# A third result tile, two semaphores for the adding stores and a new order of loads in the Strassen loop of a float32 encoder kernel

## The chip, the cores and the metric

The kernel runs on one core of one Trainium2 chip, as a single launch. The metric is the device time of one execution in microseconds. Five engines work side by side: TensorE (PE, its weight loads are listed as PEld), VectorE (DVE), ScalarE (ACT), GpSimd (POOL) and SyncE (SP). SP does nothing but ask for transfers and wait; POOL asks for some transfers too. Everything is float32. PE takes its operands as pairs of a high and a low part, and three matmuls (high by high, high by low, low by high) make one product.

## The reference

Two layers over a residual stream of 2048 tokens by 1024 channels. What matters here is the second, odd layer, cut to this:

```python
h = rms_norm(x, g_pre[l]) * (1.0 + scale) + shift
p = h @ w_in_o                      # 1024 -> 3 * 2048: u, v and the gate z
uv, z = gelu(p[..., :4096]), p[..., 4096:]
u, v = uv[..., :2048], layer_norm(uv[..., 2048:], g_ln, b_ln)
mixed = einsum('gij,bnjgc->bnigc', w_s, chunks_of_128(v)) + b_s
y = (u * mixed * silu(z)) @ w_out_o # 2048 -> 1024
x = x + gate * rms_norm(y, g_post[l])
```

## The kernel before

The first layer (projections, gated linear attention, latent attention, output projection) fills the first half of the run and is not touched. Then come two parts of the second layer.

**The v part** (`v_sp`, `v_act`, `v_dve`, `v_pe`) computes v in four column blocks of 512 (n = 0 to 3) by sixteen tiles of 128 tokens (p = 0 to 15). For each tile PE makes 24 matmuls, ACT takes the result out of PSUM with a GELU into one of four slots of the ring `vev` (L2439), DVE takes statistics from it, and SP stores it to memory (L2404). ACT may write a slot only when the store of four tiles earlier has landed. In the last block (n = 3) SP also asks for the first four pieces of weights of the next part (`pair_load`, issued at L2825, waiting at its head for `s_tqs`). That semaphore tells that POOL has finished `part_sums` and `out_sums`: sums of input and weight blocks for the Strassen scheme, done on POOL in the meantime. From p = 9 on SP asks for the first input sums (`part_load`, L2780).

**The Strassen part** (`uz_sp`, `uz_pool`, `uz_act`, `uz_dve`, `uz_pe`) does the other two projections and the output projection with seven block products in place of eight. It has four stages h = 0 to 3: h = 0 and 1 compute u and z, with 16 units each, h = 2 and 3 compute y in two halves of the sum, with 8 units each. A unit j = (h, i, u) is seven products k = 0 to 6 of 12 matmuls, 128x512 each (L3219 to L3221). While PE is in unit j, ACT and POOL make the high and low parts of the weights of the unit after it, product by product (`pair_hi` L2852, `pair_lo` L2856), after POOL has built three sums of the four weight pieces (`pair_sums`, L2830 to L2833) and later a fourth (`pair_last`, L2838). SP loads the pieces in the order 0, 1, 2, 3; piece 2 may be asked for when POOL has made the low part of product 4 of the weights before, and piece 3 when it has made that of product 6.

At the change of stage the input sums in `hTh` and `hTl` are replaced: 28 parts, four for each product. SP loads them through a ring of six tiles (`part_load`), ACT makes the high part (`part_hi`, L2790), DVE the low part (`part_lo`, L2795), which also frees the ring's tile. The last unit of a stage ("ending") and the first of the next ("opening") do this work; parts 12 to 15 are needed by product 3, parts 16 to 19 by product 4.

Stage h = 3 has eight units, called u0 to u7 below. Each gives two result tiles of 128 tokens by 1024 channels, s = 1 and s = 0. DVE takes products out of PSUM into the tile (L3139 and L3157 for s = 1, L3165 and L3183 for s = 0), adds the first half of the sum that SP has loaded (`add_p`, L3087; loads L2898), ACT squares them (`squares`, L3021), POOL makes the reciprocal root (`rstd`, L2969 to L2973), DVE scales the tile (`scale`, L3093), and POOL starts a transfer that adds the tile to `out` in memory (`add_out`, L2982). `free_y` makes DVE wait until the tile's last content has gone. There are two tiles, one for each s. The scratch output of `squares` is the tile `yp` into which SP loads, so that load waits for `squares`. `cnt_y(j, n)` below is n times the number of units of the stage before j.

The order on each engine is that of the code: queues are in order, and a wait holds all that stands behind it.

Of the kernel before, what the change touches and what calls it, by code (L numbers as in the profile page):

```python
# [62 lines left out]
def emit(nc, a, out):  # L63
# [16 lines left out]
    with ExitStack() as ctx:  # L80
# [2319 lines left out]
        def v_sp(sp):  # L2400
            def store(n, p):
                t = v_tile(n, p)
                sp.wait_ge(s_vev, n * NT + p + 3)
                sp.dma_start(sg_v[t * P:(t + 1) * P, ds(n * 512, 512)], vev[:, p % 4, :]).then_inc(s_vst[p % 4], 16)  # L2404
            norm_load(sp, 1, (6,))
            for t in range(4):
                store(0, t)
            norm_load(sp, 1, (7,))
            for t in range(4, 8):
                store(0, t)  # L2410
            sp.wait_ge(s_tp, 64)
            v_load(sp, 1)
            for t in range(8, NT):
                store(0, t)
            with sp.Fori(1, NV - 1) as n:
                v_load(sp, n + 1)
                for t in range(NT):
                    store(n, t)
                    rows = ds(n * (S // 2) + (t * (P // 2) - S // 2), P // 2)
                    sp.dma_start(out[rows, :], x1[rows, :]).then_inc(s_xo, 16)  # L2420
            for p in range(NT):
                store(NV - 1, p)
                if p == 0:
# [149 lines left out]
        zu3 = at("zu3", H0 + 74 * K, [P, 512])  # L2573
        y_tile = [at("y_tile%d" % t, H0 + (18 + 8 * t) * K, [P, 2, 16 * K])[:, :, 0:512] for t in range(2)]
        uT, zT = ([y[:, b, :] for b in range(2)] for y in y_tile)
        E_add = 256 + 48 * 4

        s_tq, E_tq = s_msx, 5 * NT
        s_zw = sem("s_zw")
        s_tqs, E_tqs = sem("s_tqs"), 0  # L2580
# [67 lines left out]
        def is_last(j):  # L2648
            return is_unit(j, 3, PAIRS[3] - 1, 1)
# [208 lines left out]
        def uz_sp(sp):  # L2858
# [41 lines left out]
            def unit(j):  # L2900
# [53 lines left out]
        def uz_pool(pool):  # L2954
# [20 lines left out]
            def add_out(j, s):  # L2975

                h, i, u = j
                if is_unit(j, 3, 0, 0) and s:
                    pool.wait_ge(s_xo, E_xo + 16 * 2 * NT)
                pool.wait_ge(s_tqs, E_add + cnt_y(j, 32, 16 * (1 - s)))  # L2980
                pool.wait_ge(s_oz, E_oz + cnt_y(j, 4, 4 - 2 * s))
                pool.dma_start(out[ds(i * (4 * P) + (2 * u + s) * P, P), :].rearrange("p (b c) -> p b c", b=2), y_tile[s],  # L2982
                               accum_op=ALU.add).then_inc(s_tqs, 16)

            def unit(j):
                if not is_last(j):
                    pair_sums(pool, j, 1)
                if j[0] == 3 and before(j)[0] == 3:
                    add_out(before(j), 1)
                for k in range(7):  # L2990
                    if not is_last(j):
                        pair_lo(pool, j, 1, k)
                        if k == 1:
                            pair_last(pool, j, 1)
                    if k == 0 and j[0] == 3 and before(j)[0] == 3:
                        rstd(before(j), 0)
                    if k == 3 and j[0] == 3 and before(j)[0] == 3:
                        add_out(before(j), 0)
                    if k == 4 and j[0] == 3:
                        rstd(j, 1)  # L3000
            unit_loop(pool, unit)
            final = (3, PAIRS[3] - 1, 1)
            add_out(final, 1)
            rstd(final, 0)
            add_out(final, 0)

        def uz_act(act):
# [3 lines left out]
            def squares(j, s):  # L3011
                tile = (uT, zT)[s]
                for b in range(2):
                    if s:
                        act.wait_ge(s_pa[1], E_pa + cnt_y(j, 2, 2 - b))
                    elif b:
                        act.wait_ge(s_pa[0], E_pa + cnt_y(j, 1, 1))
                    else:
                        act.wait_ge(s_c11, E_c11 + cnt(j, 1, 1 - NU_))
                        act.wait_ge(s_pa[0], E_pa + cnt_y(j, 1, 1))  # L3020
                    act.activation(yp[:, s, b * 512:(b + 1) * 512], tile[b][:, :], ACT.Square, scale=D ** -0.5,  # L3021
                                   accum_out=ossq2[:, 2 * s + b:2 * s + b + 1]).then_inc(s_osq, 1)
# [55 lines left out]
        def uz_dve(dve):  # L3078
            def add_p(j, s, b):

                y = (uT, zT)[s][b]
                dve.wait_ge(s_py[s], E_py + cnt_y(j, 16, 16))
# [6 lines left out]
            def scale(j, s):  # L3089
                dve.wait_ge(s_or, E_or + cnt_y(j, 6, 6 - 3 * s))  # L3090
                for b in range(2):
                    y = (uT, zT)[s][b]
                    dve.scalar_tensor_tensor(y[:, :], y[:, :], ors[:, s:s + 1], gate[:, 1, b * 512:(b + 1) * 512], ALU.mult, ALU.mult  # L3093
                                             ).then_inc(s_oz, 1)

            def free_y(j, s):
# [3 lines left out]
                elif j[0] == 2 or is_unit(j, 3, 0, 0):  # L3100
                    dve.wait_ge(s_ost[s], E_ost + cnt(j, 32, -32 * NU_))
                else:
                    dve.wait_ge(s_tqs, E_add + cnt_y(j, 32, -16 * s))

            def unit(j):
# [59 lines left out]
                dve.tensor_tensor(uT[1][:, :], PS[:, 6, :], zu2[:, :], ALU.add).then_inc(s_zc12, 1)  # L3165
                parts(ending, 12)
                if h == 3:
                    add_p(j, 0, 1)
                    scale(j, 1)
                if h < 2:  # L3170
# [7 lines left out]
                else:  # L3178
# [3 lines left out]
                    else:  # L3182
                        dve.tensor_tensor(uT[0][:, :], PS[:, 2 + u, :], yp[:, 0, 0:512], ALU.add).then_inc(s_c11, 1)  # L3183
                if is_unit(j, 2, 0, 1):
# [5 lines left out]
        def uz_pe(pe):  # L3190
# [33 lines left out]
            def column_sums():  # L3224
                pe.wait_ge(s_vev, NV * NT + 2)
                pe.wait_ge(s_zw, 16)
                for b in range(2):
# [27 lines left out]
        def _(sp):  # L3255
# [14 lines left out]
            sp.wait_ge(s_xo, E_xo + 16 * 2 * NT)  # L3270
            sp.wait_ge(s_tqs, E_add + 16 * NT)

# [139 lines left out]
```

## Time and profile before

| | us |
|---|---|
| median of 3 runs | 3026.44 (3021.3 to 3030.6) |
| profiled execution, its own time | 3029.56 |
| its span | 3027.7 |
| v part, last block, to the first matmul of the Strassen part | 1862 to 1964 |
| Strassen part | 1964 to 3011 |
| stage h = 3, from its first product | from 2822 |

The span runs from the first to the last instruction; the execution's own time is 1.9 us longer. PE is busy for 95% of the span, DVE 58%, ACT 47%, POOL 46%. In a list of the trace, the bracket behind an instruction tells how long its engine had been idle before it and what ended that.

### The profile page before, as it was taken

The numbers are of one execution on the slowest core, as the hardware profiler recorded it, in microseconds if no ns is written. First come the engines' busy times: TensorE is split into PE (matmuls) and PEld (weight loads), VectorE is DVE, ScalarE is ACT, GpSimd is POOL, SyncE is SP. The second block draws the span as 40 slices with busy tenths as digits, with TensorE's granted clock in tenths as the row PEclk, the third lists the DMA queues.
The fourth block names the chain that finished last, engine by engine and source line by source line (L and its number), as shares of the span: only waits on it lengthen the run. The fifth ranks groups of instructions, "written<-read, shape, count | busy, mean of one in ns | idle before, by whom it ended". The sixth has DMA issues, their size and how long they took to land.

```text
span 3027.7 us, 49891 instructions
## 1 busy us (share of the span) xinstructions
PE 2868.3 (95%) x15972; PEld 2383.0 (79%) x15972; DVE 1742.3 (58%) x2909; ACT 1413.1 (47%) x2582; POOL 1382.8 (46%) x1342
## 2 busy tenths in 40 slices
PE   4999999999999999999999999899998999979887
PEld 4768888788788888887878888688887888868675
DVE  6577777865777777773444221255457545662654
ACT  4652255554555555553244111266567556632432
POOL 0212211366333333332322764186776777667685
PEclk8999999999999999999999999999999999989999
DMA  7243355596211121114543455433225332445665
GB/s 268 67 128 103 106 162 165 178 284 187 72 56 57 58 60 57 58 56 142 176 159 135 163 186 175 144 122 109 99 97 181 106 103 97 150 153 181 205 145 106
DMA packets 309365, 397.64 MB, mean 131 GB/s; under 512 B 22820, under 2 KB 201124, under 8 KB 307143
## 3 DMA queue, kind: packets, MB, share of 16 engines
q1 hardware_dynamic: 300072, 367.50, 37.4%
q0 software_dynamic: 9152, 28.31, 3.7%
q8 instruction: 81, 1.33, 0.2%
q14 instruction: 60, 0.49, 0.1%
HBM read 265.05 MB, written 139.07 MB: 133 GB/s over the span
## 4 chain that ended last, share of the span: by engine, by line
PE 68%; POOL 9%; DMA 7%; DVE 6%; issue 6%; ACT 3%; SPq 1%; POOLq 0%; DVEq 0%; ACTq 0%
PE PS L3219 8%; PE PS L3220 8%; PE PS L3221 8%; PE PS L344 4%; PE PS L346 4%; PE PS L345 4%; POOL tq L2699 4%; PE PS L1795 4%; PE PS L1773 4%; DMA hc<-tq 2%; PE PS L1796 2%; PE PS L1763 2%; PE PS L1764 2%; PE PS L1762 2%; PE PS L1766 2%
## 5 line engine op out<-in xcount | busy, mean ns | idle before, releaser
L3219 PE MATMUL PS<-hTh,wc 128*128 128x512 f32 x1344 | 535.2, 398 | 51.0 <-DVE hTl L2795 17.5
L3220 PE MATMUL PS<-hTl,wc 128*128 128x512 f32 x1344 | 530.2, 395 | 0.0
L3221 PE MATMUL PS<-hTh,wc 128*128 128x512 f32 x1344 | 529.6, 394 | 0.0
L2856 POOL TENSOR_TENSOR wc<-wpr,wc 128x512 fp32r<-128x512 f32 x192 | 271.9, 1416 | 203.4 <-ACT wc L2852 203.3
L3219 PEld LDWEIGHTS PS<-hTh,wc 128*128 128x128 f32 x1344 | 256.5, 191 | 111.2 <-issue 37.0
L3221 PEld LDWEIGHTS PS<-hTh,wc 128*128 128x128 f32 x1344 | 256.6, 191 | 54.6
L3220 PEld LDWEIGHTS PS<-hTl,wc 128*128 128x128 f32 x1344 | 256.8, 191 | 52.6 <-issue 0.2
L344 PE MATMUL PS<-hTh,whi 128*128 128x512 f32 x640 | 257.9, 403 | 1.4 <-DVE hTl L298 1.1
L346 PE MATMUL PS<-hTh,wlo 128*128 128x512 f32 x640 | 250.4, 391 | 0.0
L345 PE MATMUL PS<-hTl,whi 128*128 128x512 f32 x640 | 250.2, 391 | 0.0
L1876 ACT ACTIVATE pb__164<-PS,nm,rq 128x512 f32<-128x512 f32 x256 | 197.4, 779 | 104.1 <-DVE nm L1939 104.1
L2856 POOL TENSOR_TENSOR wc<-wsx,wc 128x512 fp32r<-128x512 f32 x144 | 194.7, 1352 | 102.0 <-ACT wc L2852 102.0
L2041 POOL TENSOR_TENSOR diag<-ident,rinv 128x128 f32<-128x128 f32 x64 | 37.9, 592 | 390.0 <-PE PS L1783 285.2
L2523 PE MATMUL PS<-vsh,hTh 128*128 128x512 f32 x512 | 201.1, 393 | 13.8 <-ACT vev L2439 11.7
L1883 ACT ACTIVATE pt<-PS 128x512 fp32r<-128x512 f32 x256 | 139.5, 598 | 154.2 <-PE PS L1773 154.2
L334 POOL TENSOR_TENSOR whi<-wraw,zero 128x1024 fp32r<-128x1024 f32 x18 | 35.3, 1963 | 361.6 <-PE PS L346 361.6
L2524 PE MATMUL PS<-vsl,hTh 128*128 128x512 f32 x512 | 200.2, 391 | 0.0
L2525 PE MATMUL PS<-vsh,hTl 128*128 128x512 f32 x512 | 200.1, 391 | 0.0
L2479 DVE BATCH_NORM_STATS2 vst<-vev 128x6 f32<-128x512 f32 (+1 forms) x64 | 44.3, 693 | 247.0 <-ACT vev L2439 246.8
L1795 PE MATMUL PS<-pt,mvh 128*128 128x512 f32 x512 | 185.4, 401 | 1.1 <-DVE pt L1952 1.1
L1952 DVE TENSOR_TENSOR pt<-PS,pt 128x512 fp32r<-128x512 f32 x256 | 164.0, 682 | 9.8 <-ACT pt L1883 7.7
L371 ACT ACTIVATE pev<-PS 128x512 f32<-128x512 f32 x80 | 47.7, 596 | 258.0 <-PE PS L346 257.4
(320 smaller groups left out, 6919.9 us busy)
## 6 DMA issues: line engine op xcount, KB each, us to landing
wpr<-wuz SPq DMA_DIRECT2D x128, 256.0 KB, 3.4
projT<-pev SPq DMA_DIRECT2D x80, 256.0 KB, 2.7
xt<-x SPq DMA_DIRECT2D x8, 2048.0 KB, 8.5
mw<-wmod SPq DMA_DIRECT2D x64, 256.0 KB, 2.8
sg_v<-vev SPq DMA_DIRECT2D x64, 256.0 KB, 2.7
vm<-sg_v SPq DMA_DIRECT2D x32, 512.0 KB, 3.8
sgT<-mT SPq DMA_DIRECT2D x32, 512.0 KB, 3.5
wpr<-sgT SPq DMA_DIRECT2D x64, 256.0 KB, 3.2
```

What stands on the lines that cost most here:

```text
L344: pe.matmul(PS[:, bank, :], w[1][:, s, k, :], hTh[:, k, b], start=(k == 0), stop=False)
L345: pe.matmul(PS[:, bank, :], w[1][:, s, k, :], hTl[:, k, b], start=False, stop=False)
L346: mm = pe.matmul(PS[:, bank, :], w[2][:, s, k, :], hTh[:, k, b], start=False, stop=(k == KD - 1))
L1795: pe.matmul(PS[:, 6, :], vh[:, tok], pt[:, k, :, :].rearrange("p a q -> p (a q)"), start=(k == 0), stop=False)
L1876: act.activation(pb_[:, u, blk(b)], PS[:, b, :], ACT.Exp, bias=nm[:, u:u + 1], scale=rq2[:, 0, ds(i * 2 + u, 1)], accum_out=rs4[:, u, b:b ...
L2523: pe.matmul(o, hTh[:, k, tok], vsh[:, k, :], start=(k == 0), stop=False)
L2524: pe.matmul(o, hTh[:, k, tok], vsl[:, k, :], start=False, stop=False)
L2525: mm = pe.matmul(o, hTl[:, k, tok], vsh[:, k, :], start=False, stop=(k == KD - 1))
L2856: pool.tensor_tensor(w_part(k, 1), W_SRC[k], w_part(k, 0).bitcast(F32), ALU.subtract).then_inc(s_wcl, 1)
L3219: pe.matmul(o, wc[:, k, 0, kk, :], hh, start=(kk == 0 and not onto), stop=False, skip_group_check=onto)
L3220: pe.matmul(o, wc[:, k, 0, kk, :], hl, start=False, stop=False, skip_group_check=onto)
L3221: mm = pe.matmul(o, wc[:, k, 1, kk, :], hh, start=False, stop=(kk == 3), skip_group_check=onto)
```

## The change

It has six parts.

1. In the last block of the v part, the request for the first four weight pieces moves from behind the store of tile 0 to behind the store of tile 4.
2. In the opening unit of stages 1 to 3, SP asks for piece 2 before parts 12 to 21, and for piece 3 behind them. Before, it was parts 12 to 17, pieces 2 and 3, parts 18 to 21.
3. The s = 0 tile of every second unit of h = 3 is a new tile, `y_next`. It is contiguous in its partition.
4. The adding stores have two semaphores, `s_tqs` for s = 0 and `s_yb` for s = 1, and no longer wait for one another. `free_y` waits for s = 1 of the unit before, and for s = 0 of two units before.
5. POOL starts the s = 0 add of two units before ahead of the loop over k, the s = 1 add of the unit before at k = 0 behind `pair_lo`, and `rstd` for s = 0 at k = 2.
6. DVE scales the s = 0 tile of the unit before behind the sum of the fifth product (k = 4) in place of that of the third, and scales its s = 1 tile before `add_p` of s = 0.

Also, `s_zw` becomes an old semaphore with a base of 128.

```diff
@@ v_sp
             for p in range(NT):
                 store(NV - 1, p)
-                if p == 0:
+                if p == 4:
                     pair_load(sp, (0, 0, 0), range(4), True)
@@
+        y_next = at("y_next", X0 + 52 * K, [P, 2, 512])[:, :, :]
+        def y_of(j, s):
+            return y_next if j[0] == 3 and s == 0 and j[2] else y_tile[s]
@@ uz_sp, unit
-                parts(opening, 12, 18)
                 if not is_last(j):
-                    pair_load(sp, after(j), (2, 3))
-                parts(opening, 18, 22)
+                    pair_load(sp, after(j), (2,))
+                parts(opening, 12, 22)
+                if not is_last(j):
+                    pair_load(sp, after(j), (3,))
@@ uz_pool, add_out
-                pool.wait_ge(s_tqs, E_add + cnt_y(j, 32, 16 * (1 - s)))
                 pool.wait_ge(s_oz, E_oz + cnt_y(j, 4, 4 - 2 * s))
-                pool.dma_start(out[...], y_tile[s], accum_op=ALU.add).then_inc(s_tqs, 16)
+                pool.dma_start(out[...], y_of(j, s), accum_op=ALU.add).then_inc(s_yb if s else s_tqs, 16)
@@ uz_pool, unit
-                if j[0] == 3 and before(j)[0] == 3:
-                    add_out(before(j), 1)
+                if j[0] == 3 and before(j)[0] == 3 and before(before(j))[0] == 3:
+                    add_out(before(before(j)), 0)
                 for k in range(7):
...
                     if k == 0 and j[0] == 3 and before(j)[0] == 3:
+                        add_out(before(j), 1)
+                    if k == 2 and j[0] == 3 and before(j)[0] == 3:
                         rstd(before(j), 0)
-                    if k == 3 and j[0] == 3 and before(j)[0] == 3:
-                        add_out(before(j), 0)
@@ uz_pool, end
+            add_out(before(final), 0)
             add_out(final, 1)
             rstd(final, 0)
             add_out(final, 0)
@@ uz_dve, free_y
-                else:
-                    dve.wait_ge(s_tqs, E_add + cnt_y(j, 32, -16 * s))
+                elif s:
+                    dve.wait_ge(s_yb, cnt_y(j, 16))
+                elif not is_unit(j, 3, 0, 1):
+                    dve.wait_ge(s_tqs, E_add + cnt_y(j, 16, -16))
@@ uz_dve, unit
-                if h == 3 and before(j)[0] == 3:
-                    scale(before(j), 0)
                 parts(opening, 16)
...
                 if h == 3:
                     add_p(j, 1, 0)
+                if h == 3 and before(j)[0] == 3:
+                    scale(before(j), 0)
...
                 if h == 3:
+                    scale(j, 1)
                     add_p(j, 0, 1)
-                    scale(j, 1)
```

On POOL, in a unit of the loop of h = 3 (u2), this stood in a row before: the three sums of the weight pieces (`wsx`, `wpr`), the add of s = 1 (`y_tile1`), the low part of product 0 (`wc`), the reciprocal root (`small`).

```order
L2830 TENSOR_TENSOR wsx_217<-wpr_216 128x512
L2832 TENSOR_TENSOR wsx_217<-wsx_217,wpr_216 128x512
L2833 TENSOR_TENSOR wpr_216<-wpr_216 128x512
L2982 DMA out<-y_tile1_222 256x1x512
L2856 TENSOR_TENSOR wc_207<-wpr_216,wc_207 128x512
L2969 TENSOR_TENSOR small_55<-small_55 128x1
L2971 TENSOR_TENSOR small_55<-small_55 128x1
L2973 TENSOR_TENSOR small_55<-small_55,negh_57 128x1
```

And this stands there now, at the same place (its lines are 6 to 9 higher):

```order
L2836 TENSOR_TENSOR wsx_217<-wpr_216 128x512
L2838 TENSOR_TENSOR wsx_217<-wsx_217,wpr_216 128x512
L2839 TENSOR_TENSOR wpr_216<-wpr_216 128x512
L2988 DMA out<-y_tile0_221 256x1x512
L2862 TENSOR_TENSOR wc_207<-wpr_216,wc_207 128x512
L2988 DMA out<-y_tile1_222 256x1x512
L2862 TENSOR_TENSOR wc_207<-wsx_217,wc_207 128x512
```

Two adds now stand around the first low part, the s = 1 one second; the root has gone behind the low part of product 2.

On DVE, in u1, the second unit of h = 3, the sums of products 1 to 4 (`zu`, then `y_tile1_222`, which is s = 1) stood like this before, with the scaling of s = 0 (`y_tile0_221`) among them:

```order
L3129 TENSOR_TENSOR zu3_220<-PS,zu2_219 128x512
L3093 SCALAR_TENSOR_TENSOR y_tile0_221<-y_tile0_221,small_55,gate_56 128x512 x2
L3139 TENSOR_TENSOR y_tile1_222<-PS,zu3_220 128x512
L3087 TENSOR_TENSOR y_tile1_222<-y_tile1_222,yp_224 128x512
L3157 TENSOR_TENSOR y_tile1_222<-PS,zu2_219 128x512
```

Now the scaling stands behind all of them:

```order
L3138 TENSOR_TENSOR zu3_220<-PS,zu2_219 128x512
L3146 TENSOR_TENSOR y_tile1_222<-PS,zu3_220 128x512
L3094 TENSOR_TENSOR y_tile1_222<-y_tile1_222,yp_225 128x512
L3164 TENSOR_TENSOR y_tile1_222<-PS,zu2_219 128x512
L3094 TENSOR_TENSOR y_tile1_222<-y_tile1_222,yp_225 128x512
L3100 SCALAR_TENSOR_TENSOR y_tile0_221<-y_tile0_221,small_55,gate_56 128x512 x2
L3174 TENSOR_TENSOR y_next_223<-PS,zu2_219 128x512
```

The sum of product 3, for which PE's product 5 waits, now stands directly behind that of product 2.

On SP, at the opening of stage 2 (`hst` are the ring's tiles, `hw` and `woo` the sources of the parts, `wpr` the weight pieces, two at the first place being pieces 0 and 1), before:

```order
L2825 DMA wpr_216<-sgT 128x4x128 x2
L2780 DMA hst4_205<-hw 128x512
L2780 DMA hst5_206<-hw 128x512
L2780 DMA hst0_201<-hw 128x512
L2780 DMA hst1_202<-hw 128x512
L2780 DMA hst2_203<-hw 128x512
L2780 DMA hst3_204<-hw 128x512
L2825 DMA wpr_216<-sgT 128x4x128 x2
L2780 DMA hst4_205<-hw 128x512
L2780 DMA hst5_206<-hw 128x512
```

Now:

```order
L2831 DMA wpr_216<-sgT 128x4x128 x3
L2786 DMA hst4_205<-hw 128x512
L2786 DMA hst5_206<-hw 128x512
L2786 DMA hst0_201<-hw 128x512
L2786 DMA hst1_202<-hw 128x512
L2786 DMA hst2_203<-hw 128x512
L2786 DMA hst3_204<-hw 128x512
L2786 DMA hst4_205<-hw 128x512
L2786 DMA hst5_206<-hw 128x512
```

Piece 2, with its wait for POOL, stands ahead of parts 12 to 17.

## Rows read from the trace of the kernel before

**Rows 1.** The page, part 5: the costliest group of matmuls.

```profile
L3219 PE MATMUL PS<-hTh,wc 128*128 128x512 f32 x1344 | 535.2, 398 | 51.0 <-DVE hTl L2795 17.5
```

**Rows 2.** Timeline of SP, last v block: start, duration, instruction.

```profile
1868.34 0.35 SPq L2404 DMA_DIRECT2D sg_v<-vev  x1
1905.09 1.78 SPq L2825 DMA_DIRECT2D wpr<-wuz  x4
```

**Rows 3.** Timelines of ACT (tiles 4, 5 and 9) and of PE, same stretch.

```profile
1889.48 0.60 ACT L2439 ACTIVATE vev<-PS 128x512 f32<-128x512 f32 x1 [4.84 <-PE PS L2525]
1911.42 0.60 ACT L2439 ACTIVATE vev<-PS 128x512 f32<-128x512 f32 x1 [21.34 <-DMA sg_v<-vev]
...
1931.17 0.60 ACT L2439 ACTIVATE vev<-PS 128x512 f32<-128x512 f32 x1 [4.84 <-PE PS L2525]
...
1912.07 0.80 PE L2523 MATMUL PS<-vsh,hTh 128*128 128x512 f32 x1 [11.75 <-ACT vev L2439]
```

**Rows 4.** Openings of stages 1 and 2: SP and DVE at stage 2, PE at both.

```profile
2641.87 4.77 SPq L2780 DMA_DIRECT2D hst<-hw  x6
2649.55 6.15 SPq L2825 DMA_DIRECT2D wpr<-sgT  x2
...
2650.95 3.18 DVE L2795 TENSOR_TENSOR hTl<-hst,hTh 128x512 fp32r<-128x512 f32 x4 [4.06 <-ACT hTh L2790]
...
2321.87 0.77 PE L3219 MATMUL PS<-hTh,wc 128*128 128x512 f32 x1 [7.93 <-DVE hTl L2795]
...
2666.84 0.77 PE L3219 MATMUL PS<-hTh,wc 128*128 128x512 f32 x1 [9.61 <-DVE hTl L2795]
```

**Rows 5.** Opening of stage 3: SP and PE.

```profile
2824.87 3.10 SPq L2780 DMA_DIRECT2D hst<-hw  x6
2828.01 7.58 SPq L2825 DMA_DIRECT2D wpr<-sgT  x2
2835.69 0.93 SPq L2780 DMA_DIRECT2D hst<-hw  x2
...
2844.30 0.77 PE L3219 MATMUL PS<-hTh,wc 128*128 128x512 f32 x1 [5.94 <-issue]
```

**Rows 6.** Waits of PE from 2850 us to the end: total, times, longest.

```profile
PE PS L3219 <- DVE y_tile L3139: 13.3, 5, 3.5
```

**Rows 7.** Timelines of DVE, SP and POOL in u2 and u3; DVE in u6.

```profile
2894.31 0.68 DVE L3139 TENSOR_TENSOR y_tile<-PS,zu 128x512 f32<-128x512 f32 x1
...
2913.80 3.44 DVE L3093 SCALAR_TENSOR_TENSOR y_tile<-y_tile,small,gate 128x512 f32<-128x512 f32 x2 [4.12 <-POOL small L2973]
2917.16 0.68 DVE L3139 TENSOR_TENSOR y_tile<-PS,zu 128x512 f32<-128x512 f32 x1
...
2984.88 0.68 DVE L3139 TENSOR_TENSOR y_tile<-PS,zu 128x512 f32<-128x512 f32 x1
...
2899.92 3.82 SPq L2825 DMA_DIRECT2D wpr<-sgT  x2
...
2906.07 1.62 POOL L2830 TENSOR_TENSOR wsx<-wpr 128x512 f32<-128x512 f32 x1 [2.87 <-DMA wpr<-sgT]
...
2910.26 1.11 POOL L2982 DMA_DIRECT2D out<-y_tile  x1
...
2912.18 0.67 POOL L2969 TENSOR_TENSOR small<-small 128x1 f32<-128x1 f32 x1
...
2925.78 1.29 POOL L2856 TENSOR_TENSOR wc<-wpr,wc 128x512 fp32r<-128x512 f32 x1 [1.00 <-ACT wc L2852]
```

**Rows 8.** DMA: 3012 to 3020 us in 40 slices; issues, median us to landing.

```profile
DMA  0000000000000000990589899899999998200000
...
wpr<-sgT SPq DMA_DIRECT2D x64, 256.0 KB, 3.2
...
out<-y_tile POOLq DMA_DIRECT2D x16, 512.0 KB, 5.8
```

**Rows 9.** Timeline of POOL: the last add of the program.

```profile
3019.72 1.11 POOL L2982 DMA_DIRECT2D out<-y_tile  x1 [3.49 <-DMA out<-y_tile]
```

More of the change, by code:

```diff
@@ L2574, in emit @@
         y_tile = [at("y_tile%d" % t, H0 + (18 + 8 * t) * K, [P, 2, 16 * K])[:, :, 0:512] for t in range(2)]
+        y_next = at("y_next", X0 + 52 * K, [P, 2, 512])[:, :, :]
         uT, zT = ([y[:, b, :] for b in range(2)] for y in y_tile)
         E_add = 256 + 48 * 4
+        def y_of(j, s):
+            return y_next if j[0] == 3 and s == 0 and j[2] else y_tile[s]
         s_tq, E_tq = s_msx, 5 * NT
-        s_zw = sem("s_zw")
+        s_zw, E_zw = s_ox[1], 128
+        s_yb = sem("s_yb")
         s_tqs, E_tqs = sem("s_tqs"), 0
@@ L2979, in add_out @@
                     pool.wait_ge(s_xo, E_xo + 16 * 2 * NT)
-                pool.wait_ge(s_tqs, E_add + cnt_y(j, 32, 16 * (1 - s)))
                 pool.wait_ge(s_oz, E_oz + cnt_y(j, 4, 4 - 2 * s))
-                pool.dma_start(out[ds(i * (4 * P) + (2 * u + s) * P, P), :].rearrange("p (b c) -> p b c", b=2), y_tile[s],
-                               accum_op=ALU.add).then_inc(s_tqs, 16)
+                pool.dma_start(out[ds(i * (4 * P) + (2 * u + s) * P, P), :].rearrange("p (b c) -> p b c", b=2), y_of(j, s),
+                               accum_op=ALU.add).then_inc(s_yb if s else s_tqs, 16)
             def unit(j):
@@ L3011, in squares @@
             def squares(j, s):
-                tile = (uT, zT)[s]
+                tile = y_of(j, s)
                 for b in range(2):
@@ L3020, in squares @@
                         act.wait_ge(s_pa[0], E_pa + cnt_y(j, 1, 1))
-                    act.activation(yp[:, s, b * 512:(b + 1) * 512], tile[b][:, :], ACT.Square, scale=D ** -0.5,
+                    act.activation(yp[:, s, b * 512:(b + 1) * 512], tile[:, b, :], ACT.Square, scale=D ** -0.5,
                                    accum_out=ossq2[:, 2 * s + b:2 * s + b + 1]).then_inc(s_osq, 1)
@@ L3079, in add_p @@
             def add_p(j, s, b):
-                y = (uT, zT)[s][b]
+                y = y_of(j, s)[:, b, :]
                 dve.wait_ge(s_py[s], E_py + cnt_y(j, 16, 16))
@@ L3091, in scale @@
                 for b in range(2):
-                    y = (uT, zT)[s][b]
+                    y = y_of(j, s)[:, b, :]
                     dve.scalar_tensor_tensor(y[:, :], y[:, :], ors[:, s:s + 1], gate[:, 1, b * 512:(b + 1) * 512], ALU.mult, ALU.mult
@@ L3164, in unit @@
                     free_y(j, 0)
-                dve.tensor_tensor(uT[1][:, :], PS[:, 6, :], zu2[:, :], ALU.add).then_inc(s_zc12, 1)
+                dve.tensor_tensor(y_of(j, 0)[:, 1, :], PS[:, 6, :], zu2[:, :], ALU.add).then_inc(s_zc12, 1)
                 parts(ending, 12)
                 if h == 3:
+                    scale(j, 1)
                     add_p(j, 0, 1)
-                    scale(j, 1)
                 if h < 2:
@@ L3182, in unit @@
                     else:
-                        dve.tensor_tensor(uT[0][:, :], PS[:, 2 + u, :], yp[:, 0, 0:512], ALU.add).then_inc(s_c11, 1)
+                        dve.tensor_tensor(y_of(j, 0)[:, 0, :], PS[:, 2 + u, :], yp[:, 0, 0:512], ALU.add).then_inc(s_c11, 1)
                 if is_unit(j, 2, 0, 1):
@@ L3225, in column_sums @@
                 pe.wait_ge(s_vev, NV * NT + 2)
-                pe.wait_ge(s_zw, 16)
+                pe.wait_ge(s_zw, E_zw + 16)
                 for b in range(2):
@@ L3270, in _ @@
             sp.wait_ge(s_xo, E_xo + 16 * 2 * NT)
-            sp.wait_ge(s_tqs, E_add + 16 * NT)
+            sp.wait_ge(s_tqs, E_add + 8 * NT)
+            sp.wait_ge(s_yb, 8 * NT)
         @block.gpsimd
```

## The prediction, made before the result was known

> **What bounds the kernel now.** I read the page first. The costliest matmul group is that of the Strassen part, with 51.0 us of idle time before it [rows 1]. PE is busy nearly everywhere, so what can be won lies in its gaps, and I looked for them in the timeline, from the v part on. Three places bear on the change.
>
> The last v block: PE stands still for 11.75 us, released by an eviction of ACT; ACT itself had been idle for 21.34 us and waited for a store [rows 3]. SP shows why. It issues the store of tile 0 at 1868.34 and the weight pieces only at 1905.09: for 36 us it stands at the wait for POOL's sums, with the stores of tiles 1 to 15 behind it [rows 2]. The ring of four is full after tile 4.
>
> The openings: PE is idle for 7.93, 9.61 and 5.94 us before product 4 of stages 1, 2 and 3 [rows 4, 5].
>
> Stage 3: five waits, 13.3 us in all, for L3139, the sum of product 3 [rows 6]. From u2 to u6 L3139 comes every (2984.88 - 2894.31)/4 = 22.64 us [rows 7], of which PE waits 13.3/5 = 2.7. It is a loop. L3139 at 2894.31 leads over add_p, squares and SP to the request for piece 2 at 2899.92; it has landed when POOL's sums start at 2906.07; 4.19 us later the s = 1 add is issued, then a low part, the root (from 2912.18), the scaling on DVE (from 2913.80), and L3139 at 2917.16 [rows 7]. I call the start of the sums S and that of L3139 X: S to X is 11.09, X to S 11.76.
>
> **Part 1, the request behind tile 4.** Stores 1 to 4 leave at once, so tiles 5 to 8 find their slots free. Tile 9 needs the store of tile 5, which SP issues behind the pieces at 1905.09 + 1.78 = 1906.9. The pace is 4.84 + 0.60 = 5.44 us a tile, so tile 9 is evicted at 1889.48 + 5 x 5.44 = 1916.68 instead of 1931.17 [rows 2, 3]. Gain 14.5 us: the wait, and the slower matmuls behind it (the first takes 0.80 us). What follows is paced by these tiles, so all of it moves. The slack is about 6 us (1916.7 less some 4 for store and landing, against 1906.9); if POOL's sums end later than that, the gain shrinks one for one.
>
> **Part 2, the openings.** Piece 2 could not leave earlier than it did: SP reached it after the six parts, 2641.87 + 4.77 = 2646.6, and issued it at 2649.55 [rows 4], so it waited for POOL, not for the parts. Now the parts wait too, and part 12 leaves at 2650.0 in place of 2641.87. Landing takes about 4.5 us, as between the requests from 2835.69 on and part 18 or 19 of stage 3 [rows 5]. DVE makes parts 12 to 15 from 2650.95 to 2654.1 [rows 4]; now some 4.5 us later. Behind them DVE has four products of the gate, and these lose less since POOL is later too: I take +2.1 of the 4.5 for product 4, and by the same steps +1.8 at stage 1 (bounds 0, if DVE catches up, and 4 each). At stage 3 the six parts leave quickly, 2824.87 to 2828.0, and piece 2 at 2828.01: now they leave 2.7 later. But part 18 stood behind piece 3, at 2835.69 [rows 5], and now needs only a free ring tile, about 1.3 us earlier; it leads to product 4 at 2844.30. I take -1.6 (bounds -3 and +2.7). Together +2.3.
>
> **Parts 3 to 6, the loop.** The root and the scaling leave the path from S to X. What is late next is `free_y` for s = 1: the add of the unit before must have landed. It is issued not at 4.19 but behind another add and a low part, at 4.19 + (2912.18 - 2910.26) = 6.11 [rows 7]. An add alone takes 5.8 us from issue to landing, and for some 3.8 of them, 3015.2 to 3019, the 16 DMA engines are 80 to 99% busy [rows 8]. The trace shows no two adds at once. Bounds: beside the first one, X = S + 6.11 + 5.8 = 11.9; fully behind it, with 0.8 for the weight piece that goes beside them (half the bytes, at most half of the 3.8), S + 4.19 + 5.8 + 3.8 + 0.8 = 14.6. Busy engines speak for the second. For every other add of s = 0 the source is contiguous, which may shorten the first. I take 14.0 on average, near the second bound: +2.9 against 11.09.
>
> X to S gets shorter: the request for piece 2 took 6.15 us beside an add (by the order in the code the s = 0 add went out at k = 3, just ahead of the low part that releases the piece). No add is in flight there now. The median over the run is 3.2 [rows 8], and the load for `yp` still goes ahead of it, so I take 4. Then POOL is next: its low part of product 6 ended at 2925.78 + 1.29 = 2927.07, 9.9 after X [rows 7], and PE's longer gap makes that 10.5. So X to S is 10.5, -1.3. A round costs +1.6, and there are five (u2 to u6): +8.0. Bounds: 11.9 + 10.3 = 22.2, -0.4 x 5 = -2, and 14.6 + 11.9 = 26.5, +3.8 x 5 = +19. The scaling on DVE and the early release of the s = 0 tile are worth nothing: they hang off the loop.
>
> The Trainium skill, "DMA: Bandwidth & Descriptors", section "Anatomy of one DMA — SWDGE (gpsimd) path", gives 2.0 us and the bytes over 436 GB/s; for 512 KB that would be 3.2 us, an estimate, and 1.2 of queue for a second one. The trace disagrees: 5.8 and 3.8 [rows 8]. The same page, section "Two DMAs through the same engine are not ordered", says that descriptors start in order but are pipelined; that speaks for the first bound and is the first rival.
>
> **The end.** The last add waited 3.49 us at 3019.72 for the one before to land [rows 9]. Without that wait it follows the scaling, at about 3017.9: -1.8. Its own landing stays.
>
> **Sum**, on the profiled 3029.56: -14.5 + 2.3 + 8.0 - 1.8 = -6.0, 3023.6. The median of the runs, 3026.4, is 3.1 below that execution, so 3020.4.
>
> **Rivals.**
>
> *The adds overlap.* X = S + 11.9, the loop gains 2 in all instead of losing 8.0: -14.5 + 2.3 - 2 - 1.8 = -16, 3010.4. For it: a busy share does not tell whether an engine could have a second packet under way. Against it: the busy engines [rows 8]. It decides if the second add lands before S + 12.5. Chance 0.25.
>
> *The loop takes all back.* The second add waits fully and piece 2 stays at 6.15, since the load for `yp` ahead of it remains: 26.5 a round, +19; -14.5 + 2.3 + 19 - 1.8 = +5; PE's gaps of 6 us bring slower matmuls as at 1912.07 and 2844.30, and with openings at their upper bounds (+7) it is about +12, 3038. It is slower from +3.5 a round on, that is if the second add lands later than S + 15. Chance 0.13.
>
> *The v stall stays.* If the sums end past 1911 because the stores now share the transfers with them; at full length it leaves +9, 3035. Chance 0.04.
>
> *The openings cost nothing*: 3018.1. Chance 0.10.
>
> *The forecast*, chance 0.48, with its own range 3015 to 3028.
>
> **Numbers.** No change within 0.3%, 9.1 us, can be told from noise: faster means below 3017.3, slower above 3035.5. Faster takes nearly all of the first rival and a little of the forecast and the fourth: 0.33. Slower takes half of the second and some of the third: 0.09, and I allow 0.11. Same 0.56. The range, 3010 to 3035, reaches to the first rival's time and to the last two's.
>
> **What would show it.** Step 1: no gap of PE in the last v block, tile 9's eviction 27.2 us behind tile 4's. Step 2: idle time before product 3 at stages 1 and 2, and product 4 later by about 2 us. Step 3: L3139 released by the add of s = 1, issue to landing near 9 us on the second of a pair, rounds of 24 to 24.5 us; 22.3 would be the first rival, 26 the second. Step 4: the last two adds without a wait between them. The forecast is wrong if the rounds are shorter than before, or if PE still waits for a store of v.

## The result, and the profile after

In 20 runs of each, the changed kernel took 3028.57 us (median; 3023.9 to 3035.2) and the kernel before 3023.20 us (3016.8 to 3031.9): a ratio of 1.0018, with a 95% interval of 1.0010 to 1.0027. That is 5.4 us slower. The prediction said 3020.4, 6.0 below before, in a range of 3010 to 3035. The time lies in the range and inside the 0.3% called "no change", but it went the other way. The profiled execution of the changed kernel took 3031.48 us, with a span of 3029.8 (before: 3029.56 and 3027.7). So the two traces lie 1.9 us apart where the medians lie 5.4 apart: that of before is of an execution 6.4 us above its kernel's median, that of the changed kernel 2.9 above.

The page, part 5, the same group of matmuls as in [rows 1]. Its idle time rose from 51.0 to 63.4 us, and what ends most of it is now the sum of product 3, L3146 (L3139 before):

```profile
L3228 PE MATMUL PS<-hTh,wc 128*128 128x512 f32 x1344 | 538.9, 401 | 63.4 <-DVE y_tile L3146 19.9
```

**The last v block.** Timelines of SP and ACT, the answer to [rows 2, 3]:

```profile
1868.33 16.65 SPq L2404 DMA_DIRECT2D sg_v<-vev  x4
1901.12 1.78 SPq L2831 DMA_DIRECT2D wpr<-wuz  x4
...
1889.46 0.60 ACT L2439 ACTIVATE vev<-PS 128x512 f32<-128x512 f32 x1 [4.84 <-PE PS L2525]
1916.66 0.60 ACT L2439 ACTIVATE vev<-PS 128x512 f32<-128x512 f32 x1 [4.84 <-PE PS L2525]
```

The stores leave as their tiles come, the pieces follow behind tile 4, and tile 9 is evicted at 1916.66, 27.20 behind tile 4. The first matmul of the Strassen part starts at 1949.8 in place of 1964.3.

**The openings.** SP and DVE at the opening of stage 2, then the first matmul of product 4 at stages 1, 2 and 3, as in [rows 4, 5]:

```profile
2630.81 9.89 SPq L2831 DMA_DIRECT2D wpr<-sgT  x3
2640.75 2.88 SPq L2786 DMA_DIRECT2D hst<-hw  x6
...
2646.43 2.63 DVE L2801 TENSOR_TENSOR hTl<-hst,hTh 128x512 fp32r<-128x512 f32 x4 [9.88 <-ACT hTh L2796]
...
2310.36 0.77 PE L3228 MATMUL PS<-hTh,wc 128*128 128x512 f32 x1 [6.44 <-DVE hTl L2801]
...
2661.68 0.77 PE L3228 MATMUL PS<-hTh,wc 128*128 128x512 f32 x1 [8.00 <-DVE hTl L2801]
...
2837.69 0.77 PE L3228 MATMUL PS<-hTh,wc 128*128 128x512 f32 x1 [3.29 <-POOL wc L2862]
```

The three weight pieces are one group on SP, the last of them held until about 2640.3, and parts 12 to 17 start behind it. DVE now stands still for 9.88 us where it did for 4.06. Of the 14.5 us won in the v part, 11.5 are left at product 4 of stage 1 and 5.2 at that of stage 2. The shorter idle time in the row mustn't mislead: part of the wait has only moved ahead of product 3, where a gap of 5.04 us is new at stage 2.

**The loop of stage 3.** Waits of PE from 2850 us on, for [rows 6], then DVE and POOL in u3, for [rows 7]:

```profile
PE PS L3228 <- DVE y_tile L3146: 19.9, 6, 4.2
```

```profile
2891.05 0.69 DVE L3146 TENSOR_TENSOR y_tile<-PS,zu 128x512 f32<-128x512 f32 x1 [7.30 <-DMA out<-y_tile]
...
2915.51 0.69 DVE L3146 TENSOR_TENSOR y_tile<-PS,zu 128x512 f32<-128x512 f32 x1 [7.70 <-DMA out<-y_tile]
...
2966.78 0.69 DVE L3146 TENSOR_TENSOR y_tile<-PS,zu 128x512 f32<-128x512 f32 x1 [8.06 <-DMA out<-y_tile]
...
2991.21 0.69 DVE L3146 TENSOR_TENSOR y_tile<-PS,zu 128x512 f32<-128x512 f32 x1 [6.26 <-DMA out<-y_tile]
...
2901.10 1.29 POOL L2836 TENSOR_TENSOR wsx<-wpr 128x512 f32<-128x512 f32 x1
...
2904.96 0.91 POOL L2988 DMA_DIRECT2D out<-y_next  x1
...
2906.84 1.43 POOL L2988 DMA_DIRECT2D out<-y_tile  x1
```

Every L3146 from u1 on is released by the landing of an add; before, none was. Take S and X as in the prediction. In u3 POOL's sums start at 2901.10 (S), the first add goes at 2904.96, the second at 2906.84, and X is 2915.51: S + 14.4, and 8.67 from the second issue. Over u2 to u6 S to X is 14.3 on average, X to the next S 10.6. From u1 (2866.73) to u6 (2991.21) the five rounds take 124.5 us; before they took 113.0 (from 2871.93 to [rows 7]). The page's list of DMA issues, for [rows 8], shows the landing of the adds at 7.1 us in the median, from 5.8:

```profile
out<-y_tile POOLq DMA_DIRECT2D x12, 512.0 KB, 7.1
```

**TensorE's clock.** Stretches of the loop: length, busy times of PE, PEld, DVE, ACT and POOL, granted clock (1.00 is 2.4 GHz, 0.50 is 1.2 GHz), DMA share, GB/s. First before, u1 to u7, then after: u1 to u7, and the part of u3 behind X.

```profile
2872.00:3004.00 132.00, 118.75 (x498) 96.09 (x498) 67.65 (x80) 42.77 (x92) 107.74 (x109) 0.96 0.60 134
```

```profile
2867.00:3010.00 143.00, 124.64 (x499) 100.67 (x500) 60.06 (x78) 41.77 (x91) 100.20 (x107) 0.92 0.53 122
2915.00:2922.00 7.00, 5.74 (x14) 4.49 (x15) 4.13 (x7) 1.48 (x5) 1.65 (x4) 0.52 0.19 51
```

A mean of 0.96 over 132 us is (1 - 0.96) x 2 x 132 = 11 us at the lower level; 0.92 over 143 us is 23. Behind the longer gaps of PE the products run at half speed for up to 7 us, and POOL, which waits for them through ACT, is busy for 1.65 of the 7. The two rounds with such a long stretch (behind X of u3 and of u5) have the longest X to S, 11.21 both; the others have 10.05 to 10.34. Experiments 3 and 6 below have one stretch of 7 us in their loop each, and there X to S is 11.3, in their other rounds 9.3 to 10.2. The length of the gap alone does not tell: u4 has the longest gap, 4.17 us, and a stretch of 3.5 us.

**The end.** The last add, for [rows 9]: it follows its scaling without a wait for another add.

```profile
3022.42 0.90 POOL L2988 DMA_DIRECT2D out<-y_next  x1 [1.75 <-DVE y_next L3100]
```

From L3146 of u6 to this add it takes 31.2 us, 3.6 less than before. The steps of the two traces add up to the place of the last add: -14.5 (v part), +9.3 (openings, to X of u1), +11.5 (five rounds) and -3.6 (behind them) are +2.7, and the last add goes at 3022.42 in place of 3019.72.

### The profile page after: what moved, and what is told of

It reads as the page before. It is cut to its first block, busy times and chain, and to the rows that moved or that the text cites. A ratio compares the mean times of both kernels' runs of the same rounds, so it can differ in the third digit from the quotient of the medians.

```text
span 3029.8 us, 49875 instructions
## 1 busy us (share of the span) xinstructions
PE 2873.3 (95%) x15972; PEld 2386.9 (79%) x15972; DVE 1741.3 (57%) x2909; ACT 1412.5 (47%) x2582; POOL 1377.7 (45%) x1342
## 4 chain that ended last, share of the span: by engine, by line
PE 76%; issue 6%; DVE 5%; POOL 5%; DMA 3%; ACT 3%; SPq 1%; POOLq 0%; DVEq 0%; ACTq 0%
PE PS L3228 8%; PE PS L3229 8%; PE PS L3230 8%; PE PS L344 4%; PE PS L346 4%; PE PS L345 4%; PE PS L1795 4%; PE PS L1773 4%; PE PS L2523 3%; PE PS L2524 3%; PE PS L2525 3%; PE PS L1796 2%; PE PS L1763 2%; PE PS L1764 2%; PE PS L1762 2%
## 5 line engine op out<-in xcount | busy, mean ns | idle before, releaser
L3228 PE MATMUL PS<-hTh,wc 128*128 128x512 f32 x1344 | 538.9, 401 | 63.4 <-DVE y_tile L3146 19.9
L2858 ACT ACTIVATE wc<-wpr 128x512 fp32r<-128x512 f32 x192 | 119.8, 624 | 105.4 <-PE PS L3230 104.2
```

Source lines behind the costliest of these rows:

```text
L3228: pe.matmul(o, wc[:, k, 0, kk, :], hh, start=(kk == 0 and not onto), stop=False, skip_group_check=onto)
```

## The experiments

Ratios are to the kernel before on the same chip, with 95% intervals. A per cent is 30 us; a difference between two kernels of these tables has an interval of about 0.2%, or 6 us. So times rank the larger effects, and the traces give the sizes of the small ones. A trace is one execution, though, and can lie some way from its kernel's median; where that matters it is said.

**1. Part 1 alone.**

```diff
-                if p == 0:
+                if p == 4:
                     pair_load(sp, (0, 0, 0), range(4), True)
```

> The kernel before with part 1 alone (the four weight pieces asked behind the store of tile 4). Both theories: the v part ends 14.5 us earlier and nothing takes it back, so -14.5 against before, ratio 0.9952. Rival: the stages behind it wait for something that did not move (the openings, or the sums that fill the ring), and part of the 14.5 is lost again; then less than -10.

Measured: 0.9957 (0.9940 to 0.9973), -13 us. Nothing takes the 14.5 back, and the five rounds are as before (22.2 to 23.0 us each, PE waits 13.4 us for L3139). So the rest of the change cost some 18 us.

**2. Parts 1 and 2.** The order of requests is that of the diff above, on the kernel before.

> Parts 1 and 2 (tile 4, and the new order of requests at the openings), the loop of stage 3 as before. The forecast's step for the openings, +2.3, gives -12.2 against before. The reading of the two traces (product 4 lost 3.0 at stage 1, 6.35 at stage 2, and some 2 at stage 3, with 2.9 gained between) gives some +9 for the openings and so -5.5. Ratio 0.9960 by the one, 0.9982 by the other.

Measured: 0.9976 (0.9962 to 0.9990), so the openings cost 0.19%, 5.7 us: above the forecast's 2.3, below the 9 read from one pair of traces, and with an interval of 6 it excludes neither. The trace has the same picture as after (product 4 of stage 2, 350.4 us behind that of stage 1):

```profile
2632.76 9.62 SPq L2825 DMA_DIRECT2D wpr<-sgT  x3
...
2647.66 2.75 DVE L2795 TENSOR_TENSOR hTl<-hst,hTh 128x512 fp32r<-128x512 f32 x4 [9.16 <-ACT hTh L2790]
...
2663.03 0.77 PE L3220 MATMUL PS<-hTh,wc 128*128 128x512 f32 x1 [7.95 <-DVE hTl L2795]
```

**3. All but part 2.** The changed kernel with `parts(opening, 12, 18)`, pieces 2 and 3, `parts(opening, 18, 22)` again.

> The changed kernel with the old order of requests at the openings (part 2 undone), the new loop of stage 3 kept. The forecast: 2.3 us faster than the changed kernel, so -8.3 against before from its own terms. The reading of the traces: 9 us faster than the changed kernel; -14.5 + 11.5 for the five rounds - 3.6 behind them = -6.6 against before. What would speak against both: no gain over the changed kernel, that is a cost of the openings that is hidden behind the loop.

Measured: 0.9996 (0.9982 to 1.0011), -1 us: both expectations against before, -8.3 and -6.6, missed, and both lie outside the interval. Against the changed kernel (1.0018) that gives the openings 0.22%, 6.7 us, a second time. Against experiment 1 the loop and the end cost 0.39%, 11.8 us with an interval of 6; from the changed kernel and experiment 2 it is 12.7. Its own trace gives less. X from u1 to u6 takes 122.0 us in place of 113.0 (before) and 113.2 (experiment 1), and from X of u1 to the last add it is 155.0, against 147.8 and 148.8: 6 to 7 us. The forecast's terms, 8.0 - 1.8 = 6.2, are inside the interval, at its lower edge. One reason for the difference is that this trace is not of a typical execution. The twelve times fall into four of 3014.6 to 3018.5 us and eight of 3024.2 to 3031.7; the trace is of one of 3014.92, 10.5 below the median. What the eight slower ones do otherwise, no trace shows.

**4. The adds exchanged.** S = 1 first, right behind the sums; s = 0 of two units back at k = 2, behind a wait for an event a round back. Old openings.

```diff
-                if j[0] == 3 and before(j)[0] == 3 and before(before(j))[0] == 3:
-                    add_out(before(before(j)), 0)
+                if j[0] == 3 and before(j)[0] == 3:
+                    add_out(before(j), 1)
...
-                    if k == 0 and j[0] == 3 and before(j)[0] == 3:
-                        add_out(before(j), 1)
+                    if k == 2 and j[0] == 3 and before(j)[0] == 3 and before(before(j))[0] == 3:
+                        pool.wait_ge(s_zc12, E_zc12 + cnt(before(j), 1, 1))
+                        add_out(before(before(j)), 0)
```

> As the run before it, but the s = 1 add is issued right behind POOL's sums again, and the s = 0 add of two units back follows at k = 2 (with a wait for an event that lies a round back, to keep the order of adds and of the writes to their tiles). Theory: L3146 waits for the landing of the s = 1 add, and what makes it late in the changed kernel is the other add ahead of it in the queue. Then S to X falls from 14.3 to about 4.2 + 7.0 = 11.2, the round from 24.9 to about 21.8, and the loop costs -4 in place of +11.5: -14.5 - 4 - 2 = -20 against before, ratio 0.993. Rival: the s = 0 add only collides elsewhere (with piece 2 and the load for yp, which lead to the next S): X to S grows from 10.6 to 13 or more, the round stays at 24 or more, and the time is that of the run before it.

Measured: 0.9922 (0.9906 to 0.9938), 22 us faster than experiment 3, which differs by this order (and that wait). S to X falls to 11.9, X to S is 9.8, and u1 to u6 takes 108.8 us, 21.8 a round as expected. Of the 2.1 us by which S to X falls against experiment 3, 1.5 are the place on POOL (the s = 1 add leaves 4.3 us behind S, in experiment 3 5.8) and 0.6 the way from issue to X (7.7 on average, from 8.3). PE waits for L3147 in four places:

```profile
PE PS L3229 <- DVE y_tile L3147: 10.7, 4, 3.3
```

The trace explains 155.0 - 141.6 = 13.4 of the 22 us (X of u1 to the last add); the interval of the difference reaches from 16 to 29. The two traces can't settle it: that of experiment 3 lies 10.5 us below its median and this one 4.6 above, and at product 4 of stage 2, ahead of all that differs, this one is already 6.4 us later. The cause is shown all the same: the add that goes first, by the room that it takes on POOL and by its transfer, makes X late.

**5. The s = 1 add ahead of the sums.** `add_out(before(j), 1)` moved above `pair_sums(pool, j, 1)`.

> As e4_swap_adds, but the s = 1 add is issued ahead of POOL's sums in place of behind them. In e4_swap_adds L3147 still waits for this add (idle 3.5 to 7.3 us, round 21.8), and the scaling that it needs has ended by the time the sums start (DVE at 2911.2, sums at 2911.19; DVE at 2932.3, sums at 2934.05). If the landing of that add is the last link, it moves forward by 4.2 less its own issue of 1.1 on POOL: S to X 8 to 9 in place of 11.9, X to S 11 in place of 9.8, and PE becomes the bound, at about 20 a round: 5 x 1.8 = 9 us faster than e4_swap_adds, about 2995. Rival: POOL is the bound of X to S, and what it waits for the scaling and spends on the issue comes back one for one; then the round stays at 21.5 or more and the time within 3 us of e4_swap_adds.

Measured: 0.9934 (0.9920 to 0.9949), the same as experiment 4. From u3 on S to X is 5.1 and X to S 14.9 to 16.9: S to X loses 6.8 us and X to S gains most of it; ahead of each of these adds POOL waits 1.2 to 1.9 us for the scaling. The time is the rival's, though the five rounds of the trace are 4 us shorter (104.5 in place of 108.8). The trace is also of use as a measurement. No other add is under way beside this one, and no weight piece is requested behind it, only the load for `yp`, 2.1 us later; it takes 5.7 to 5.95 us from issue to X (u3 to u6). And PE never falls to the lower clock here, with gaps of 1.5 us at most in this stretch:

```profile
2857.00:2983.00 126.00, 119.09 (x517) 96.02 (x515) 76.99 (x78) 42.34 (x93) 112.01 (x112) 1.00 0.57 133
```

**6. Half of the first add.** In experiment 3's kernel the first add of each round carries `[:, 0:512]` only; the other half of those rows of `out` is left out.

> As e3_v_loop, but the s = 0 add that goes first in each round of the loop carries half of its columns (256 KB in place of 512; left out: the other half of those rows of out). It asks what the second add waits for. If the data phases follow one another, half of the first one's 3.8 us goes: S to X falls from 14.4 to about 12.5, the round from 24.4 to 22.6. If the first add costs a fixed time of the queue, or if POOL's issue is what counts, nothing changes: S to X stays at 14 or more. Only the profile is needed.

Measured in its profile: from the second issue to X 7.4 to 8.8 us, on average 8.1; in experiment 3 it is 8.3. S to X is 13.9 against 14.1. Halving the first add changes next to nothing there, so the picture of two data phases in a row, each as long as its bytes, fails. The time, 0.9977 (0.9963 to 0.9992), is 6 us below experiment 3's with an interval of 6, and leaves this open. The row is that of u3; the second add left at 2902.47:

```profile
2910.71 0.69 DVE L3149 TENSOR_TENSOR y_tile<-PS,zu 128x512 f32<-128x512 f32 x1 [7.10 <-DMA out<-y_tile]
```

**7. Piece 3 alone moved back.** On experiment 1's kernel, with the old loop.

```diff
                 parts(opening, 12, 18)
                 if not is_last(j):
-                    pair_load(sp, after(j), (2, 3))
+                    pair_load(sp, after(j), (2,))
                 parts(opening, 18, 22)
+                if not is_last(j):
+                    pair_load(sp, after(j), (3,))
```

> As e1_v_only (old loop), but at the openings piece 3 alone is moved behind parts 18 to 21; piece 2 stays behind parts 12 to 17. It parts the two moves that part 2 makes. Theory: what costs at stages 1 and 2 is that parts 12 to 17 stand behind piece 2, which waits for POOL; so product 4 comes at its old distance there (345 to 347.5 us from the one of stage 1 to the one of stage 2, against 350.4 and 351.3 with the new order) and the time is that of e1_v_only within 2 us, or up to 2 less. Rival: the late piece 3 holds POOL's last sum and the products behind it; then the distances are those of the new order, and the time is 5 to 7 us over e1_v_only, like e2_v_openings.

Measured: 0.9959 (0.9943 to 0.9975), as experiment 1. Product 4 of stage 2 comes 346.1 us behind that of stage 1. The six parts leave early again and DVE waits half as long:

```profile
2626.37 4.46 SPq L2780 DMA_DIRECT2D hst<-hw  x6
2634.52 0.38 SPq L2825 DMA_DIRECT2D wpr<-sgT  x1
...
2635.94 3.17 DVE L2795 TENSOR_TENSOR hTl<-hst,hTh 128x512 fp32r<-128x512 f32 x4 [4.85 <-ACT hTh L2790]
```

So the cost of part 2 is parts 12 to 17 behind piece 2, and the later piece 3 is free. Whether it helps at stage 3 is not clear: from product 4 of stage 2 to X of u1 it takes 200.0 us here against 201.8 in experiment 1, and 200.7 against 201.5 in experiments 9 and 8, but 203.3 against 202.7 in experiments 10 and 4.

**8. The s = 0 root and add earlier.** Experiment 5 with `rstd(before(j), 0)` at k = 0 and the s = 0 add at k = 1.

> As e5_early_add, but POOL computes the root for s = 0 at k = 0 (in place of k = 2) and issues the s = 0 add of two units back at k = 1. In e5_early_add POOL waits 1.2 to 1.9 us for the scaling of s = 1 ahead of the early add; DVE is late with it because it waited 3.2 us for the s = 0 root. Theory: X to S, now 15 to 16.5 us, loses these 1.2 to 1.9 us, the round goes from 21.6 to about 20.2, and the kernel is 6 to 8 us faster than e5_early_add. Rival: the root of s = 1 is the later one (POOL computes it at k = 4, behind the squares), so the scaling of s = 1 comes as before; the round stays within 0.5 of 21.6 and the time within 3 us.

Measured: 0.9923 (0.9909 to 0.9936), against experiment 5's 0.9934. The rounds from u3 on take 21.0 to 21.5 us, not 20.2, and POOL still waits 1.2 us for the scaling of s = 1: the rival holds in the time. Its reason, the later root of s = 1, holds in part. In experiment 5 the scaling of s = 1 started 0.6 to 2.6 us behind the end of its root, held by what stood ahead of it on DVE, so there the root did not set the pace. In u3 to u5 of this kernel it starts right at the root's end, with DVE free only 0.01 to 0.2 us before. And the second instruction of the earlier s = 0 scaling takes 4.8 to 5.0 us here, where it took 1.8 there.

**9. That, with the order of experiment 7.**

> As e8_root_early, with the order of e7_three_before_four at the openings (parts 12 to 17, piece 2, parts 18 to 21, piece 3). From product 4 of stage 2 to L3139 of unit 1 of stage 3, e7 took 200.0 us and the kernels with the old order 201.8 to 205.1, so it should be 2 us faster than e8_root_early; within noise (4 us) of it in any case. A loss of more than 4 us would say that the last weight piece holds the new loop.

Measured: 0.9906 (0.9891 to 0.9921), 2997.5 us, the fastest of the series, 28 us or 0.94% below the kernel before; against experiment 8 it is 5 us, with an interval of 6, where 2 were expected. From u2 to u6 X comes every 21.1 us, with no time at the lower clock. One early add and its wait for the scaling, then X 5.7 later:

```profile
2906.68 1.14 POOL L2989 DMA_DIRECT2D out<-y_tile  x1 [1.23 <-DVE y_tile L3103]
2907.36 1.78 POOL L2836 TENSOR_TENSOR wsx<-wpr 128x512 f32<-128x512 f32 x1
...
2912.40 0.69 DVE L3149 TENSOR_TENSOR y_tile<-PS,zu 128x512 f32<-128x512 f32 x1 [3.78 <-DMA out<-y_tile]
```

**10. Experiment 4 with the order of experiment 7.**

> e4_swap_adds with the openings of e7_three_before_four. Again 2 us faster than e4_swap_adds by the trace (0.9922 of before), so about 0.9915; beside the run before it this asks which place of the s = 1 add is the better one: by e4 and e5 they are equal within noise, though the loop of e5 is 1.9 us shorter in its trace.

Measured: 0.9927 (0.9913 to 0.9942). The 2 us do not show; it is the same as experiment 4 within the interval.

**11. A tiny first add.** As experiment 6 with 16 columns, 8 KB; the other columns are left out.

> As e6_half_first_add, but the first add of a round carries 16 columns (8 KB in place of 512; left out: the other columns of those rows of out). In e3_v_loop the second add takes 7.5 to 8.9 us from issue to the wait's end, in e6_half_first_add 7.4 to 8.8, and alone, in e5_early_add, 5.7 to 6.0. If an add ahead costs a fixed time in the queue whatever its size, the second takes 7 to 8.5 here too and S to X stays at 13 or more. If its bytes are what delays the second one, and the half one was too large still to be out of the way, issue to end falls to 6 to 7 (a piece of the weights goes beside it), S to X to 12.0 or less, and PE's gap to under 2.5. Only the profile is needed.

Measured in its profile: from the second issue to X 6.1 to 6.3 us in four of five rounds (7.7 in u5), S to X 11.9 to 12.5 there. An add ahead costs no large fixed time, then (6.2 against 5.7 to 5.95 in experiment 5, with a weight piece beside it here); it costs by what it carries, but not in proportion. The time says the same: 0.9949 (0.9931 to 0.9967), 14 us below experiment 3, of which the trace has 10 in the five rounds. The two issues of u3, and X:

```profile
2895.49 0.89 POOL L2988 DMA_DIRECT2D out<-y_next  x1
2897.38 1.42 POOL L2991 DMA_DIRECT2D out<-y_tile  x1
...
2903.64 0.69 DVE L3149 TENSOR_TENSOR y_tile<-PS,zu 128x512 f32<-128x512 f32 x1 [6.61 <-DMA out<-y_tile]
```

## Why the prediction was wrong

It had four terms on the profiled execution: -14.5, +2.3, +8.0 and -1.8. In the traces they came out as -14.5, +9.3, +11.5 and -3.6. The steps that failed are the sizes of two terms, the openings by 7.0 us and the loop by 3.5; the end gave 1.8 back, and a gain of 6.0 became a loss of 2.7 in the traces, 5.4 in the medians.

**Part 1, -14.5: right.** Tile 9 27.2 us behind tile 4 was the sign named in advance. The trace gave 14.5, experiment 1 -13. (In the twelve kernels with part 1 the first matmul of the Strassen part starts between 1945.9 and 1952.3, 12 to 18 us before the 1964.3 of before: one pair of traces gives such a size to some 3 us only.)

**Part 2, +2.3: this step failed.** The mechanism was the one given, parts 12 to 17 waiting with piece 2 (experiment 7 shows it), and so was the size of the first link, "some 4.5 us later": DVE starts parts 12 to 15 5.5 us later than in experiment 1, measured from product 4 of stage 1. What failed is the sentence "these lose less since POOL is later too: I take +2.1 of the 4.5". DVE has its four products of the gate right behind these parts and the next four parts behind those, without a pause, so nearly the whole delay goes on to product 4: 345.9 us between products 4 of stages 1 and 2 on average over before and experiments 1, 3 and 4, 350.9 over the changed kernel and experiment 2, +4.9. (Over all eleven kernels with piece 2 behind the parts it is 346.7, from 344.9 to 347.9.) At stage 1, from the first Strassen matmul, it is +3.0 by the same kernels. Together that is 7.9, where the upper bounds, 4 each, give 8. Stage 3 was forecast to gain 1.6 and lost: from product 4 of stage 2 to X of u1 takes 205.7 us with the new order, and 202.9 on average over before and experiments 1, 3 and 4, of which before has 205.1; so the loss is not clear of the spread, but the forecast gain is not there. Nor is a gain of the earlier part 18 clear (experiment 7). These averages sum to 10.7 us, the one pair of traces to 9.3, the two timed pairs to 5.7 and 6.7, each with an interval of about 6. That is 3 to 8 us more than forecast; the timed pairs alone don't exclude 2.3, the traces do.

**Parts 3 to 6, +8.0: right mechanism, size too small.** "X = S + 14.0" was 14.3, "X to S 10.5" was 10.6, the second add (forecast: "near 9 us", though 14.0 - 6.11 is 7.9) took 7.5 to 9.3, on average 8.5, and the two adds went out with one low part between them. The five rounds measured +11.5 in place of 8.0 in the changed kernel, +9.0 in experiment 3. Some 1.5 of the missing 3.5 us is a slip in the sum: "+1.6" compares 14.0 + 10.5 = 24.5 with 11.09 + 11.76 = 22.85, the one round of [rows 7], while the mean round of before, which the prediction quotes and uses for its bounds, is 22.6. With it the forecast round costs +9.5 in five. The other 2 are the round itself, 24.9 in place of 24.5. What the sum had no term for is the clock: the gap that PE has at product 5 grew from 2.7 to 19.9/6 = 3.3 us on average and was followed by the lower level for 23 us in place of 11, and in the two rounds where it lasted 7 us X to S was 1.0 longer. Without that the mean X to S would have been 10.2. The prediction mentioned slower matmuls only under its second rival. How much of the 12 us of the timed pairs is this, the runs do not say: the traces account for 6 to 9 of them from X of u1 to the last add.

The working behind "14.0" fitted at its ends and not between them. Its second bound put a whole data phase of 3.8 us for the first add ahead of the second, and the figure taken was 2.1 above what the second add would need alone, "11.9". Taking away all but 8 KB of the first add gave about that back, 8.3 - 6.2 = 2.1 us from issue to X (experiments 3 and 11). But half of the bytes should by the second bound's own sum have given back up to 1.9, and gave 0.2 (experiment 6). That 14.0 came so near is in part luck. The contiguous source of every other first add shows no gain: behind it the second add took 8.7 and 9.1 us, behind the others 8.2, 9.3 and 7.5.

The Trainium skill, "DMA: Bandwidth & Descriptors", section "Anatomy of one DMA — SWDGE (gpsimd) path", gives bytes over 436 GB/s for the data, 1.2 us for 512 KB, an estimate. The runs differ: experiment 3 against experiment 11 has 2.1 for it. Its 3.2 us for the whole add, an estimate too, stands against 5.7 to 5.95 measured in experiment 5.

**The end, -1.8: right in kind, too small.** The wait of 3.49 us is gone. From L3146 of u6 to the last add it took 3.6 us less than before; in experiment 3, whose loop is the same, 1.9 less.

**The rivals.** The adds do not overlap enough to help; experiment 4 shows what it would have been worth. The second rival set its threshold at +3.5 us a round; it was +2.3, and its other condition, openings at their upper bounds, came true at stages 1 and 2. (Its "+7" for them was itself too small: the bounds 4 + 4 + 2.7 are 8.4 above the 2.3 in its sum.) What happened lies between the forecast and this rival, and no case of its own stood there: both first sizes, of the openings and of a round, were off in the same direction.

## What to carry to other kernels

When two transfers are put into one queue, look at which of them a loop waits for, and issue that one first: here the exchange of two adds takes a round from 24.4 to 21.8 us (experiments 3 and 4). When a request is moved ahead of others on an in-order engine, price the others with the whole wait of the one moved, and take off nothing for the engines behind unless the trace shows them idle there. Where a change makes PE's gaps longer, read the granted clock behind the gaps of this length that are there already, and add the slow stretch to the sum. And take the round before and the round after from the same average.

## What the runs showed of the hardware

An accumulating DMA of 512 KB from POOL takes 5.7 to 5.95 us from issue to the wait's end when only the load for `yp` goes beside it, asked for 2.1 us behind it (experiments 5 and 9), 6.1 to 6.3 behind a tiny one (7.7 in one round), 7.4 to 8.8 behind one of 256 KB and 7.5 to 8.9 behind one of 512 KB (experiments 11, 6 and 3, weight pieces beside it). So the delay by the one ahead is not in proportion to its bytes. An add behind may cost as well. In experiments 4 and 10 none goes ahead of the s = 1 add, and the s = 0 add leaves 6.2 to 6.3 us behind it. In seven of ten rounds the s = 1 add took 7.6 to 8.4 us; in the other three, where it landed before the other left or within 0.3 us of it, 6.1 to 6.6. Whether the add behind delayed it, or only met one that was late already, the runs do not say.

The windows give a hint to the first point: in experiment 5 the first microsecond of data of an add, and one two microseconds later, then the same two for the last add of the kernel before, when no engine has an instruction left (columns as above).

```profile
2957.30:2958.30 1.00, 0.16 (x1) 0.19 (x2) 0.69 (x1) 0.74 (x4) 0.92 (x2) 1.00 0.91 63
2959.30:2960.30 1.00, 1.00 (x6) 0.79 (x5) 0.00 (x0) 0.62 (x1) 1.00 (x2) 1.00 1.13 207
```

```profile
3021.20:3022.20 1.00, 0.00 (x0) 0.00 (x0) 0.00 (x0) 0.00 (x0) 0.00 (x0) 0.50 1.12 61
3023.20:3024.20 1.00, 0.00 (x0) 0.00 (x0) 0.00 (x0) 0.00 (x0) 0.00 (x0) 0.50 1.10 203
```

The DMA engines are about as busy in the first of each pair (0.91 against 1.13, 1.12 against 1.10) and move less than a third (63 against 207 GB/s, 61 against 203). If each add begins with such a stretch, half an add costs more than half; that this is the cause is not shown, and why it is so stays open. Open too is where the rest of the timed difference between experiments 3 and 4 lies, 22 us against 13.4 in the traces, since experiment 3's trace is of one of its faster executions.
